# A seventh expert slot, row scales carried with the rows, and two products for the half-filled token tile

## What is computed

```python
m = mixer(rmsnorm(h, norm_mix), ...)       # x @ w_in; short conv and gated linear attention; @ w_o
h = h + m
xn = rmsnorm(h, norm_ffn)
g = softmax(xn @ w_group_router + b_g)     # top 1 of 4 groups
e = softmax((xn @ w_expert_router + b_e)[group])   # top 2 of its 8 experts
y = sum over the two experts of weight * ((silu(xn @ w_gate[e]) * (xn @ w_up[e])) @ w_down[e])
out = rmsnorm(h + y, norm_final)
```

## Time and profile before

| | us |
|---|---|
| median of 3 runs | 912.97 |
| lowest, highest | 912.2, 913.56 |
| profiled execution, whole | 913.54 |
| its span | 911.4 |
| PE busy | 790.4 (87%) |
| DVE busy | 293.0 (32%) |
| ACT busy | 236.8 (26%) |
| POOL busy | 78.2 (9%) |
| chain that ended last: PE, DMA, SP's queue | 72%, 9%, 8% |
| DMA moved | 173.58 MB, mean 190 GB/s |

### The profile page before, as it was taken

One profiled execution on the slowest core, in us unless ns is written; L12 is line 12 of the kernel. 1 busy time (PEld: TensorE's weight loads), 2 busy tenths in 40 slices (PEclk: granted clock), 3 DMA queues, 4 the chain that ended last, 5 costly groups with the idle time before them and its releaser, 6 DMA issues.

```text
span 911.4 us, 12524 instructions
## 1 busy us (share of the span) xinstructions
PE 790.4 (87%) x5314; PEld 639.5 (70%) x5314; DVE 293.0 (32%) x509; ACT 236.8 (26%) x347; POOL 78.2 (9%) x121
## 2 busy tenths in 40 slices
PE   4999979999999999999999989955899888788740
PEld 3998979999988899999999989952333233233210
DVE  6224142566445461222464533342100000000007
ACT  5226232555311134322222210310312111111102
POOL 2000000000202210000000000111011100100003
PEclk8999989999999999999999989966999999898975
DMA  8412112011435443221224191188999999999726
GB/s 230 143 47 93 47 46 93 1 47 50 140 112 178 146 140 93 92 94 50 89 82 162 47 338 55 48 346 333 382 411 410 410 408 409 408 408 406 295 106 223
DMA packets 82180, 173.58 MB, mean 190 GB/s; under 512 B 11986, under 2 KB 49362, under 8 KB 81556
## 3 DMA queue, kind: packets, MB, share of 16 engines
q1 hardware_dynamic: 75140, 154.79, 46.5%
q0 software_dynamic: 6992, 18.10, 5.3%
HBM read 162.35 MB, written 17.86 MB: 198 GB/s over the span
## 4 chain that ended last, share of the span: by engine, by line
PE 72%; DMA 9%; SPq 8%; DVE 5%; ACT 3%; issue 2%; POOL 1%; POOLq 0%; DVEq 0%; ACTq 0%
PE ps L1536 52%; PE ps L1839 8%; DMA wgu<-w_up 7%; SPq L396 5%; PE ps L1856 3%; SPq L401 3%; PE ps L1638 1%; PE ps L1831 1%; PE ps L1696 1%; DMA xg<-moe_rows,slots 1%; PE ps L1685 1%; PE ps L1777 1%; PE ps L1652 1%; PE ps L1650 1%; PE ps L1649 1%
## 5 line engine op out<-in xcount | busy, mean ns | idle before, releaser
L1536 PE MATMUL ps<-xh,wh 128*128 128x288 f32 x832 | 184.2, 300 | 4.0 <-ACT hist L792 2.0
L1536 PE MATMUL ps<-xl,wh 128*128 128x288 f32 x832 | 181.7, 297 | 0.0
L1536 PE MATMUL ps<-xh,wl 128*128 128x288 f32 x832 | 181.5, 297 | 0.0
L1839 PE MATMUL ps<-wgu,gx 128*64 128x512 f32 x512 | 130.3, 667 | 27.6 <-DMA wgu<-w_up 26.5
L999 DVE TENSOR_TENSOR wl<-raw,wh 128x2048 fp32r<-128x2048 f32 x36 | 82.5, 2292 | 195.1 <-ACT wh L702 195.0
L1536 PEld LDWEIGHTS ps<-xh,wh 128*128 128x128 f32 x832 | 135.6, 190 | 8.2 <-issue 5.1
L1536 PEld LDWEIGHTS ps<-xl,wh 128*128 128x128 f32 x832 | 135.9, 190 | 0.0
L1536 PEld LDWEIGHTS ps<-xh,wl 128*128 128x128 f32 x832 | 135.7, 190 | 0.0
L1839 PEld LDWEIGHTS ps<-wgu,gx 128*64 128x64 f32 x512 | 44.1, 152 | 112.3 <-issue 110.8
L702 ACT CAST wh<-raw 128x2048 fp32r<-128x2048 f32 x36 | 68.6, 1905 | 59.5 <-PE ps L1536 59.5
L1480 DVE TENSOR_TENSOR hm<-si,ps 128x256 f32<-128x256 f32 x16 | 6.7, 421 | 227.8 <-ACT si L934 227.8
(11 more groups left out here) (296 smaller groups left out, 924.9 us busy)
## 6 DMA issues: line engine op xcount, KB each, us to landing
wgu<-w_gate SPq DMA_DIRECT2D x32, 1024.0 KB, 13.8
wgu<-w_up SPq DMA_DIRECT2D x32, 1024.0 KB, 20.3
wd<-w_down SPq DMA_DIRECT2D x32, 1024.0 KB, 20.2
raw<-w_in SPq DMA_DIRECT2D x26, 1024.0 KB, 5.3
raw<-w_gla_out SPq DMA_DIRECT2D x4, 1024.0 KB, 5.3
raw<-w_o SPq DMA_DIRECT2D x4, 1024.0 KB, 5.3
y<-moe_results SPq DMA_DIRECT2D x4, 1024.0 KB, 8.0
xin<-x_prompt SPq DMA_DIRECT2D x4, 512.0 KB, 6.1
```

Source lines behind the costliest of these rows:

```text
L1536: last.append(mm(out, left(a, k), right(b, k, o), start=k == 0 and n == 0, stop=k == k_tiles - 1 and n == 2))
L1839: ins = mm(ps[half * B:(half + 1) * B, bank, :].rearrange("t (n c) -> t n c", n=2), x[:, k, half * B:(half + 1) * B], w[half][:, :, :].rea ...
```

## The change

Four edits in one.

1. **Last token tile in two products.** For the fifth tile the unused 64 columns of the high part (`xh`, `mh`) hold the low part of the same 64 tokens. One matmul with `wh` gives high x high on partitions 0 to 63 and low x high on 64 to 127; one with `wl` adds high x low. The consumer adds the two halves: in V, ACT copies them apart and POOL adds; in WO, DVE adds twice.
2. **Rows unscaled, the scale carried along.** `normed` is gone. `h` has 16 more columns (`DX`), POOL writes the row's scale into column D, and stores the raw rows. `norm_ffn` is applied by ACT on the transposed block (eight operations with a scale per partition), the row's scale in silu and in the product for `hm`. The gather's buffer is thus held until `hm`.
3. **Loads by halves.** `gate` and `up` come in two DMAs of 512 KB each, with semaphores of their own; `gate_up` is split in two halves of 16 matmuls (`gu_half`, `gu_full`), and SP refills a half when it is used.
4. **Seven slots.** Seven places overlap `h`, so the residual is read back from `moe_rows` to `hf` behind the last weights. Three experts are loaded before WO's groups end, parts of 3 and 4 within it. `nlb` is loaded last.

```diff
-SLOTS = 6
+SLOTS = 7
+DX = D + 16
+        vlo = sb("vlo", [ND, D], at=zone_q - 4 * D)
-        slot_at = [zone_a, zone_a + SLOT, zone_p, zone_p + SLOT, zone_v, zone_v - SLOT]
+        slot_at = [zone_a, zone_a + SLOT, zone_v - SLOT, zone_p, zone_p + SLOT, zone_v, zone_v + SLOT]
+        hf = sb("hf", [P, NT, D], at=slot_at[4])
...
-        def load_gate_up(eng, e):
+        def load_gate_up(eng, e, a, ns=(0, 1)):
 
-            for n, w in enumerate((w_gate, w_up)):
-                eng.dma_start(wgu[e % SLOTS][:, n, :].rearrange("p (a c) -> p a c", a=KD // RB),
-                              rows_of(w, e)).then_inc(gu_in[e % SLOTS], 16)
+            for n in ns:
+                eng.dma_start(wgu[e % SLOTS][:, n, a * HALFW:(a + 1) * HALFW],
+                              rows_of((w_gate, w_up)[n], e)[:, a, :]).then_inc(gu_in[a][e % SLOTS], 16)
...
-            sp.wait_ge(w_used, G_WO)
-            sp.dma_start(nfb[:, :], norm_ffn.to_broadcast((P, D))).then_inc(nf_in, 16)
...
-            for e in range(SLOTS):
-                if e == 2:
-                    sp.wait_ge(w_used, G_END)
-                if e == SLOTS - 1:
-                    sp.wait_ge(lg_full, NT)
-                    for i in range(XN2):
-                        sp.wait_ge(x2_out[i], 16 * ((NT - 1 - i) // XN2 + 1))
-                load_gate_up(sp, e)
+            sp.wait_ge(w_used, G_WO)
+            for e in range(3):
+                load_gate_up(sp, e, 0)
+                load_gate_up(sp, e, 1)
                 load_down(sp, e)
-            for i in range(SLOTS // 2, NP):
-                sp.wait_ge(gu_full, i - SLOTS // 2 + 1)
-                for e in (2 * i, 2 * i + 1):
-                    load_gate_up(sp, e)
-                sp.wait_ge(dn_full, i - SLOTS // 2 + 1)
-                for e in (2 * i, 2 * i + 1):
+            sp.wait_ge(lo_ready, G_END)
+            for a in range(2):
+                load_gate_up(sp, 3, a)
+            sp.wait_ge(w_used, G_END - 1)
+            for a in range(2):
+                load_gate_up(sp, 4, a, (0,))
+            sp.wait_ge(w_used, G_END)
+            for a in range(2):
+                load_gate_up(sp, 4, a, (1,))
+            load_down(sp, 4)
+            sp.wait_ge(lg_full, NT)
+            load_down(sp, 3)
+            for a in range(2):
+                load_gate_up(sp, 5, a)
+            load_down(sp, 5)
+            sp.wait_ge(rows_out, 16 * NT)
+            for a in range(2):
+                load_gate_up(sp, 6, a)
+            load_down(sp, 6)
+            for i in range((NE - SLOTS + 1) // 2):
+                refill = [e for e in (2 * i + SLOTS, 2 * i + SLOTS + 1) if e < NE]
+                sp.wait_ge(gu_half, i + 1)
+                for e in refill:
+                    load_gate_up(sp, e, 0)
+                sp.wait_ge(gu_full, i + 1)
+                for e in refill:
+                    load_gate_up(sp, e, 1)
+                sp.wait_ge(dn_full, i + 1)
+                for e in refill:
                     load_down(sp, e)
...
+            sp.dma_start(hf[:, 0:NPT, :], rows_d[0:SEQ, 0:D].rearrange("(n p) d -> p n d", p=P)).then_inc(hf_in, 16)
+            sp.dma_start(hf[0:ND, NPT, :], rows_d[SEQ:T, 0:D]).then_inc(hf_in, 16)
+            sp.dma_start(nlb[:, :], norm_final.rearrange("(a d) -> a d", a=1).to_broadcast((P, D))
+                         ).then_inc(nl_in, 16)
...
+            pool.wait_ge(unit_free[1], N_G // 2)
+            pool.tensor_tensor(v[0:ND, NPT, :], v[0:ND, NPT, :], vlo[:, :], ALU.add).then_inc(vd_ready, 1)
...
-                rms(NT + NPT + 1 + i, 16 + i, 17 + i, D, ND if i == NPT else P)
-                if i >= 1:
-                    store_rows(i - 1)
-            store_rows(NT - 1)
+                n = ND if i == NPT else P
+                rms(NT + NPT + 1 + i, 16 + i, 17 + i, D, n, h[0:n, i, D:D + 1])
+                store_rows(i)
...
-                    pool.wait_ge(xgt_full, i - GX + 1)
+                    pool.wait_ge(hm_ready, i - GX + 1)
...
+                    if t == NPT:
+                        c(copy(v[0:ND, t, cols], ps[0:ND, 2 * u, 0:256]))
+                        copy(vlo[:, cols], ps[ND:P, 2 * u, 0:256]).then_inc(unit_free[u], 1)
...
+            def scaled_block(dst, ready):
+
+                for k in range(KD):
+                    ins = act.activation(dst[:, k, :], ps[:, TB + k // 4, (k % 4) * P:(k % 4 + 1) * P], ACT.Copy,
+                                         scale=nf4[:, k:k + 1])
...
                 act.wait_ge(xgt_full, i + 1)
+                if i == 1:
+                    act.wait_ge(xinfo_ready, 1)
                 if i >= 2:
                     act.wait_ge(gu_full, i - 1)
-                copy(gx[i % 2][:, :, :], ps[:, TB:TB + 2, :].rearrange("p a (k t) -> p (a k) t", t=P)).then_inc(gx_ready, 1)
+                scaled_block(gx[i % 2], gx_ready)
...
             block_t(0)
+            silu(0)
             block_t(1)
-            silu(0)
...
+                if i == NPT:
+                    c(tt(xh[:, :, T:TP], x, high, ALU.subtract))
...
+                        tt(mh[:, one, T:TP].rearrange("p a t -> p (a t)"), tmp[u][:, SEQ:T],
+                           mh[:, one, SEQ:T].rearrange("p a t -> p (a t)").bitcast(F32), ALU.subtract)
...
+                    if t == NPT:
+                        hv = h[0:ND, t, k * 256:(k + 1) * 256]
+                        c(tt(hv, hv, ps[0:ND, 2 * u, 0:256], ALU.add))
+                        c.sync()
+                        tt(hv, hv, ps[ND:P, 2 * u, 0:256], ALU.add).then_inc(h_ready, 1)
...
-                        normed(t - 1)
...
-                tt(hm[i % 2][:, :], si[:, :], ps[:, i % 2, DE:2 * DE], ALU.mult).then_inc(hm_ready, 1)
+                stt(hm[i % 2][:, :], ps[:, i % 2, DE:2 * DE], xg[i % GX][:, D:D + 1], si[:, :], ALU.mult,
+                    ALU.mult).then_inc(hm_ready, 1)
...
+                if t == NPT:
+                    for k in ks:
+                        mm(ps[:, 2 * u, 0:256], x[0][:, k, SEQ:TP], w[0][:, k, :], start=k == 0, stop=False,
+                           skip_group_check=True)
+                        ins = mm(ps[0:ND, 2 * u, 0:256], x[0][:, k, SEQ:T], w[1][:, k, :], start=False, stop=k == KD - 1,
+                                 skip_group_check=True)
+                    return ins
...
+                w = [wgu[e % SLOTS] for e in (2 * i, 2 * i + 1)]
+                for a, done in enumerate((gu_half, gu_full)):
+                    for e in (2 * i, 2 * i + 1):
+                        pe.wait_ge(gu_in[a][e % SLOTS], 32 * (e // SLOTS + 1))
+                    gate_up(i % 2, gx[i % 2], w, range(a * RB, (a + 1) * RB)).then_inc(done, 1)
```

More of the change, by code:

```diff
@@ L153, in build @@
         nfT = sb("nfT", [P, KD])
+        nf4 = sb("nf4", [P, KD])
         xinfo = sb("xinfo", [1, XB + 1], I32)
@@ L164, in build @@
         raw = [sb(f"raw{i}", [P, GW]) for i in range(2)]
-        wh = [sb(f"wh{i}", [P, GW], F32R) for i in range(2)]
-        wl = [sb(f"wl{i}", [P, GW], F32R) for i in range(2)]
+        wh, wl = [], []
+        for i in range(2):
+            wh.append(sb(f"wh{i}", [P, GW], F32R))
+            wl.append(sb(f"wl{i}", [P, GW], F32R))
         zone_a = place[0]
@@ L240, in build @@
         assert place[0] <= zone_v + 2 * 4 * KD * TP
[L242 to L249, removed]
+        xr = [sb(f"xr{i}", [P, KD, P], at=None if i else zone_p + 2 * 4 * GW) for i in range(2)]
+        assert place[0] <= zone_p + 3 * 4 * GW
+        io = sb("io", [P, NT, NE], at=zone_b + 4 * D)
         ig = sb("ig", [P, NT, NG])
@@ L342, in build @@
         xg_in = [sem(f"xg_in{i}") for i in range(GX)]
-        gu_in = [sem(f"gu_in{i}") for i in range(SLOTS)]
+        gu_in = [[sem(f"gu_in{a}_{i}") for i in range(SLOTS)] for a in range(KD // RB)]
+        gu_half = sem("gu_half")
         wd_in = [sem(f"wd_in{i}") for i in range(SLOTS)]
@@ L567, in carry, with rms @@
                 return pool.tensor_tensor(ms[:, 29:30], expo[:, 0:1], expo[:, 0:1], ALU.add)
-            def rms(n, lo, hi, size, rows=P):
+            def rms(n, lo, hi, size, rows=P, out=None):
                 pool.wait_ge(sq_done, n + 1)
@@ L659, in _ @@
                 pool.wait_ge(y_out[p], 16 * NP // 2)
[L660 removed]
+            pool.wait_ge(hm_ready, NP)
             with pool.If(nx > 0):
@@ L933, in silu @@
                     act.wait_ge(hm_ready, i)
-                act.activation(si[:, :], ps[:, i % 2, 0:DE], ACT.Silu).then_inc(si_ready, 1)
+                act.activation(si[:, :], ps[:, i % 2, 0:DE], ACT.Silu,
+                               scale=xg[i % GX][:, D:D + 1]).then_inc(si_ready, 1)
             def result(i):
@@ L961, in _ @@
                         act.wait_ge(e_xt, j + 1)
-                        copy(gx[0][:, :, :], ps[:, TB:TB + 2, :].rearrange("p a (k t) -> p (a k) t", t=P)).then_inc(e_gx, 1)
+                        c.enter(j, KD - 1)
+                        scaled_block(gx[0], e_gx)
+                        c.leave(XP)
                         act.wait_ge(e_gu, j + 1)
```

(7 more changed lines are left out.)

126 lines of the change are left out of this document (63 added, 63 removed).

## The result

The changed kernel takes 898.42 us (median; 898.23 to 900.05) against 913.26 of the kernel before on the same chip: a ratio of 0.984, with a 95% interval of 0.981 to 0.986. The forecast was 896.3, the range 889 to 903. The profiled execution took 900.05 us, 13.5 less than the 913.54 against which the sum was made, where the sum has 17.2: the direction and most steps held, and one step was too small. It is the slowest of the four executions; by the medians the change is worth 14.8 us.

A forecast was written before the change was run, and what follows sets the result against it. PE was taken to bound the first half, the stream of expert weights the MoE. Restart -9.7, one expert less ahead -9.0, new pause +2.0 and tail -0.5 gave -17.2 us: 913.54 to 896.3, range 889 to 903.

The forecast's parts named there:

- Front: V stage, output stage and the step between, up to `slots`: 3.3 - 0.2 + 3.7 = 6.8 us earlier.
- Gather and first `gate_up`: Start of the MoE: first gather -0.5 us, eight scaled ACT copies +1.3; `gate_up` of pair 0 starts at 620.4.
- DMA idle from about 612: Sign that the forecast is right, ahead of pair 0's restart: DMA idle from about 612 to 626.
- rival (3): More than forecast: gather in 4 us (-3), no new pause (-2), full clock in last pair (-1.3): 890.0; chance 0.14.
- Restart: Weight stream restarts when half of pair 0's `gate_up` is done, at 626.3 against 635.98: -9.7 us in all.
- The new pause: Weight stream before `down` of pair 0 ends, near 641.3: empty about 2 to 3 us; +2, ends 0 and +5.
- a clock that falls further in the first pairs: Sign that the forecast is wrong, in the MoE's first pairs; no size given.
- One expert less ahead: At the restart 25 experts ahead, not 26, and `nlb` moved behind: 3.5 loads, -9.0 us, ends -8.4 to -10.0.
- Tail: From the stream's end through `gate_up` 15: -0.5 us, ends -1.8 and 0; reading back `hf` and `nlb` costs nothing.
- (1): Rival, weight stream: smaller transfers and longer rows cost at most 0.11 us a transfer, 5.5 us: 901.8; chance 0.14.
- (2): Rival, weight stream: each 512 KB transfer adds SP's issue of 0.47 us, 23.5 us: 919.8, slower than before; chance 0.05.
- (4): Rival: front gain of 6.8 us lost, the ring not being full when pair 0 is half done: 903.1; chance 0.03.

The follow-up runs named there:

- e6_pad: Changed kernel with the 8 matmuls per unit taken from the last token tile put back as useless ones: 907.37 us, ratio 0.991 to the kernel before.
- e1_full: Changed kernel, but SP refills the first halves only when the pair's whole `gate_up` is done (`gu_full`): 900.99 us, ratio 0.986.
- e2_down: Changed kernel with `down` of pair 0 put ahead of PE's transposes of pair 2: 891.23 us, ratio 0.977.
- e11_one: Changed kernel with the transposed block copied by one ACT operation instead of eight scaled ones, `norm_ffn` left out of the experts' input: 894.87 us, ratio 0.979.
- e5_down_late6: e2_down with expert 6 loaded only at the restart, after `gu_half` of pair 0: 897.83 us, ratio 0.982.
- e3_late6: Changed kernel with expert 6, the seventh slot's first tenant, loaded only at the restart, after `gu_half` of pair 0: 897.73 us, ratio 0.983.
- e8_down_whole: e4_down_full with `gate` and `up` in one DMA of 1 MB each, PE waiting for the whole: 901.78 us, ratio 0.988.
- e9_down_gather: e2_down with expert 6 issued only when the first gather has landed: 890.26 us, ratio 0.974.
- e4_down_full: e2_down with the edit of e1_full added (first halves refilled only at `gu_full`): 897.33 us, ratio 0.981.
- e13_best: e9_down_gather with `gate_up` begun on the first four scaled copies in every pair: 890.2 us, ratio 0.975.
- e12_hf2: Changed kernel with the residual rows read back twice (2.36 MB more, and a wait between): 905.18 us, ratio 0.989.

## Why the prediction was right, and the step that was too small

**Front: right.** -7.0 measured in one pair of executions, -6.8 forecast, and the first tile of two products in V takes 1.87 us (130.47 to 132.34) where a tile took 2.88 (1.92 forecast); e6_pad puts the matmuls' share at 6.8 (by the ratio) to 9.0 (by the median) where the sum had 2 x 3.84 = 7.7. Since the front alone varies by 4 us between executions, the smaller terms in it (0.5, 0.2, 0.4) are not decided by this.

**Gather and first `gate_up`: right.** +0.1 and +1.2 against -0.5 and +1.3; the gather took 7.75 us under weights that still ran at 397 GB/s between 612 and 616, where the prediction's list of signs had DMA idle from about 612. The cheap gather of rival (3) exists (4.6 us), but only where expert 6 is held back.

**Restart: right in place, wrong in worth.** 626.58 against 635.98 is -9.4 (forecast -9.7). But the sum counted every microsecond of it as one off the end. e1_full shows that the last 2.9 are worth at most 1.4 here.

**The new pause: the step that failed.** "+2, ends 0 and +5" is measured as 6.4 - 1.0 = +5.4, just past its upper end. The step has two parts: the path from `gate_up` 0 to `down` 0 was to stay at 7.8 us, and `down` 0 at its length of before. The path grew to 8.3 (638.31 - 629.97), but the larger part is `down` itself: 5.58 us against 3.65, with PE's granted clock at 0.50 after it waited 2.41 us for ACT's second block. The prediction named the longer block and the wait for `xinfo_ready` (which costs nothing), and listed a clock that falls further in the first pairs among the signs that it is wrong, but gave it no price. e2_down takes PE's wait away and gets back 6.4 us of the stretch, 5.6 without its quicker gather; e11_one gets 5.2 by making the block shorter. How much the clock costs varies: in e1_full, after a wait of 2.40 us, the same `down` takes 4.04 us, and why the clock came back sooner there stays open.

**One expert less ahead: the working holds, the size was a little smaller.** From restart to the last `yb` are 240.9 us before and 236.8 after, 4.1 less where the sum had 9.0 - 2.0 + 0.5 = 7.5. Of this 5.4 is the pause, -1.7 the tail, and the remainder, -7.8, is what is left for the loads against -9.0, just short of the lower end of 8.4; it is worked out and not measured. e5_down_late6 shows the seventh slot's three loads at +7.5 behind the start of `gate_up` 0, for 7.7 in the sum; e3_late6 shows at most 1.4 while the pause is there.

**Tail: right with the sign, small in size.** `gate_up` 15 takes 7.14 us and not 8.80: -1.7 against -0.5, within the ends. Here both halves of pair 15 ran in one piece, after a wait of 1.90 us (3.89 before), at a granted clock of 1.00 between 850 and 854 (0.68 before, between 862 and 866): the gain is the clock. Reading back `hf` and `nlb` is covered, 0.3 us before the last scatter.

**Rivals.** (1) and (2) fall by the stream's 409 GB/s and by e8_down_whole. The page "DMA: Bandwidth & Descriptors" of the Trainium skill asks for transfers of at least 1 MiB (section Bandwidth); where many are queued, no run here shows a cost of 512 KB, and the 1 MB version is 5.6 us slower. (4) falls by e6_pad. (3), 890.0, is the time that a better order reaches, for two of its reasons: the gather in 4.6 us and no pause (e9_down_gather).

The total: -9.4 (restart), -4.1 (from there to `yb`), +0.1 (end) = -13.4, and the execution shows -13.5. Of the 3.7 us that the sum had too much, 3.4 are the pause; the loads gave 1.2 us less than forecast and the tail 1.2 more, and that these two cancel is luck.

What stays open: why e1_full needs 1.4 us more from `down` 0's end than after (220.8 against 219.4). e3_late6 needs the same 220.8, but there the stream is still full when `down` 0 ends (411 and 403 GB/s), so its seven loads from the restart on begin to count. The medians of e2_down and e4_down_full differ by 6.1 where the stretches differ by 4.4; they ran on different chips, and the ratios, 0.9766 and 0.9813, differ by 4.3 us.

## What to carry to other kernels

When a ring is made longer or refilled earlier, list for each slot what frees it, and see which release is the last that the stream waits for: until that one is moved, everything gained ahead of it goes into an empty queue (the halves and the seventh slot were worth 3.9 and 7.5 us behind the first `gate_up` with the pause gone and at most 1.4 with it, and moving one call of PE bought about 6). A short wait on the matmul engine just before the operation that frees a buffer costs more than itself where the clock drops with it (16 matmuls in 5.58 us and not 3.65), so it needs a price in the sum. And to see what an edit is worth, read a stretch between two fixed events beside the median: here the front's spread of 4 us would have hidden half of the differences.

## What the runs showed of the hardware

- A gather of 128 rows of 4160 bytes lands in 4.4 to 4.6 us with no weights queued ahead (e3_late6, e5_down_late6, e9_down_gather, e13_best) and in 7.0 to 7.8 us behind them.
- In a full queue the rate doesn't hang on the piece: 409 GB/s with `gate` and `up` in pieces of 1 MB (before) and of 512 KB (after), and 0.5 us at most for 50 more transfers (e4_down_full against e8_down_whole).
- The last DMAs of a stream end unevenly: the share of the 16 engines falls from 0.96 to 0.12 in 12 us, and of a reading of 2.36 MB behind the last weights (5.8 us of bytes at 409 GB/s) 512 rows are in 14.8 us and the last 64 rows 22.3 us behind their issue (after).
- The last scatter of 128 rows takes 3.22 us alone (after) and 8.55 us beside a reading of 2.36 MB (e12_hf2).
- PE's granted clock: in pair 0 of after a wait of 2.41 us is followed by 0.50 (1.2 GHz) and 5.58 us for 16 matmuls; after waits of 1.22 us (e11_one) and 1.19 us (before), and with none (e2_down), they take 3.65 us at 1.00 (2.4 GHz). In e1_full they take 4.04 us after 2.40 us of waiting.
